# Expert weights fetched ahead in a one-core transformer block: 22 chunks for 18, expert one inside the ring, expert two outside

## What is computed

```python
def expert_choice_ffn(h, w_router, w_gate, w_up, w_down):
    b, n, d = h.shape
    cap = CAPACITY_FACTOR * n // N_EXPERTS
    aff = jax.nn.softmax((h @ w_router).astype(jnp.float32), axis=-1)
    gate, idx = lax.top_k(jnp.swapaxes(aff, 1, 2), cap)
    bidx = jnp.arange(b)[:, None, None]
    xe = h[bidx, idx]
    hid = jax.nn.silu(jnp.einsum('becd,edf->becf', xe, w_gate)) * jnp.einsum('becd,edf->becf', xe, w_up)
    ye = jnp.einsum('becf,efd->becd', hid, w_down) * gate[..., None].astype(h.dtype)
    return jnp.zeros_like(h).at[bidx, idx].add(ye)
```

## Time and profile before

| | us |
|---|---|
| median of three timed runs | 1674.55 |
| lowest, highest of them | 1671.48, 1675.87 |
| the profiled execution | 1667.71 |
| its span from first to last instruction | 1665.8 |

### The profile page before, as it was taken

The page is one execution under the profiler, slowest core; times in us unless marked ns, Lnnn a source line. Parts: engine busy times, 40 slices in busy tenths (PEclk is TensorE's granted clock), DMA queues, the critical chain, the costliest instruction groups (busy, mean ns, idle before and its releaser), DMA issues. The chain is left out here.

```text
span 1665.8 us, 26602 instructions
## 1 busy us (share of the span) xinstructions
PE 1429.2 (86%) x11146; PEld 1109.2 (67%) x11146; DVE 796.9 (48%) x1321; ACT 566.9 (34%) x821; POOL 25.2 (2%) x34
## 2 busy tenths in 40 slices
PE   5999998999968565565565599989999999999999
PEld 3889886678943121121121397549999999999999
DVE  4353336666722001000010578656776478777753
ACT  3432125675311000000000352654434366853341
POOL 1100000000000000000000000000000000200000
PEclk8999999999979877877787899999999999999999
DMA  9755447552599999999999854954545545444520
GB/s 396 310 227 219 154 168 312 213 217 102 218 382 365 428 428 428 428 427 428 427 428 428 360 220 147 383 212 144 186 178 181 188 163 177 177 172 183 178 102 26
DMA packets 48990, 437.69 MB, mean 263 GB/s; under 512 B 5232, under 2 KB 7664, under 8 KB 8304
## 3 DMA queue, kind: packets, MB, share of 16 engines
q1 hardware_dynamic: 47872, 430.99, 65.4%
q10 hardware_dynamic: 1008, 5.09, 0.7%
HBM read 435.00 MB, written 1.05 MB: 262 GB/s over the span
## 5 line engine op out<-in xcount | busy, mean ns | idle before, releaser
L796 PE MATMUL bank<-arena_r,ring_r 128*128 128x256 f32 (+1 forms) x5016 | 700.0, 285 | 12.5 <-DVE ring_end_r L1908 4.9
L796 PEld LDWEIGHTS bank<-arena_r,ring_r 128*128 128x128 f32 x5016 | 652.3, 191 | 28.3 <-issue 14.9
L1908 DVE TENSOR_TENSOR ring_r<-ring,ring_r 128x2048 fp32r<-128x2048 f32 (+1 forms) x108 | 246.0, 2280 | 154.0 <-ACT ring_r L1549 153.7
L1195 PE MATMUL bank<-ring,arena 128*32 128x512 f32 x1008 | 164.7, 785 | 117.0 <-DMA ring<-in_w 115.7
L1549 ACT ACTIVATE ring_r<-ring 128x2048 fp32r<-128x2048 f32 (+1 forms) x108 | 204.9, 1898 | 111.6 <-PE bank L796 102.9
L1195 PEld LDWEIGHTS bank<-ring,arena 128*32 128x32 f32 x1008 | 31.1, 127 | 237.4 <-DMA ring<-in_w 175.8
L796 PE MATMUL bank<-H_r,ring_r 128*128 128x256 f32 x816 | 182.4, 289 | 4.6 <-DVE H_r L1885 4.6
L796 PEld LDWEIGHTS bank<-H_r,ring_r 128*128 128x128 f32 x816 | 136.8, 195 | 8.2 <-issue 7.4
L2195 DVE TENSOR_TENSOR arena<-arena,bank 64x512 f32<-64x512 f32 x16 | 11.1, 691 | 261.4 <-ACT arena L1659 261.4
L1659 ACT ACTIVATE arena<-bank 64x512 f32<-64x512 f32 x16 | 9.4, 588 | 369.7 <-PE bank L1195 369.6
L796 PE MATMUL bank<-arena_r,ring_end_r 128*128 128x256 f32 (+1 forms) x400 | 114.3, 286 | 0.0
(11 more groups left out here) (296 smaller groups left out, 1406.0 us busy)
## 6 DMA issues: line engine op xcount, KB each, us to landing
ring<-in_w SPq DMA_DIRECT2D x93, 2048.0 KB, 25.6
ring<-in_w SPq DMA_DIRECT2D x171, 1024.0 KB, 4.9
ring_end<-in_w SPq DMA_DIRECT2D x45, 1024.0 KB, 4.9
ring<-in_bias ACTq DMA_DIRECT2D x1, 2048.0 KB, 12.4
H<-in_w SPq DMA_DIRECT2D x2, 1024.0 KB, 15.3
ring_end<-in_w SPq DMA_DIRECT2D x1, 2048.0 KB, 25.8
consts<-in_consts ACTq DMA_DIRECT2D x1, 1198.0 KB, 9.3
X<-in_x SPq DMA_DIRECT2D x1, 1024.0 KB, 5.7
```

Source lines behind the costliest of these rows:

```text
L796: i = nc.tensor.matmul(o, lhsT, rhs, start=start, stop=stop, skip_group_check=grouped)
L1195: last = matmul(bank[0][32 * j:32 * j + 32, :], x_e[:, k, CAP * e:CAP * e + CAP], columns(slot_of(c), j, 512), start=k == 0, stop=k == KT - 1)
L1908: v.tensor_tensor(r(lo), lo, r(hi), ALU.subtract).then_inc(lo_ready, 1)
```

## The change

The diff does these things.

- Four more homes, 18 to 21, all in `arena`; home 15 moves. To make room, the tiles of the routing and the gathers move within `arena` (`h_tok`, `y_tok`, `hot`, `hot_g`, `hot_t`, `aff`, `silu_g`, `hid`, `hid_t` and others).
- `EARLY` has ten entries for six. Chunks 0 to 11 of the expert stage (expert 0) lie in slots 0 to 11; chunks 12 to 21 (expert 1 without its last two) in slots 12, 13 and the eight homes; from chunk 22 on the ring turns, starting with slot 0.
- SP loads 22 chunks ahead. Six of them (homes 17 and 18 behind gate 11, the pair 10/11 and home 14 behind the last `att_t`, home 19 behind the last `att_o`) stand between the last `branch` chunk's load and the first `mix_out` chunk's. Homes 15 and 20 wait for the last `branch` product, 21 for the last `mix_out` product, 16 for the row sums as before.
- `x_e` becomes `x_first` (experts 0, 1), `x_next` (experts 2, 3) and two tiles `x_rest` (experts 4 to 15, half of the depth each, since they take the place of homes 21 and 19). `gather_next` (64 columns) stands behind each gate/up chunk of expert 1, `gather_rest` (384 columns) behind every second one of experts 2 and 3. The turn of the picks moves from expert 2 to expert 4.

The core of the diff:

```diff
-AHEAD = 2 * CAP
+AHEAD, NEXT = 2 * CAP, 4 * CAP
-SLOTS, CYCLE, HOMES = 14, 12, 4
+SLOTS, CYCLE, HOMES = 14, 12, 8
-EARLY = (12, 13) + tuple(range(SLOTS, SLOTS + HOMES))
-FIRST_CYCLE = FIRST_EXPERT + len(EARLY)
-FIRST_HOME = FIRST_EXPERT + CYCLE - len(EARLY)
+EARLY = (12, 13, 17, 18, 14, 19, 15, 20, 16, 21)
+FIRST_HOME = FIRST_EXPERT + CYCLE
+FIRST_CYCLE = FIRST_HOME + len(EARLY)
...
-            return {14: consts[:, 384:384 + CHUNK], 15: room(8448, CHUNK), 16: H[:, :, T:2 * T], 17: H[:, :, 0:T]}[s]
+            return {14: consts[:, 384:384 + CHUNK], 15: room(6144, CHUNK), 16: H[:, :, T:2 * T], 17: H[:, :, 0:T],
+                    18: room(13312, CHUNK), 19: room(11264, CHUNK), 20: room(4096, CHUNK), 21: room(0, CHUNK)}[s]
...
-        h_tok, x_e, y_tok = room(0, 2, D), room(2048, KT, EXPERTS * CAP), room(6400, 4, D)
+        h_tok, y_tok = room(8192, 2, D), room(3072, 4, D)
+        x_first, x_next = room(2048, KT, AHEAD), room(2560, KT, NEXT - AHEAD)
+        x_rest = [room(at, 4, 512 - NEXT) for at in (0, 11264)]
...
-            rounds(1)
-
+            first_mix = CHUNK_NO[("mix_out", 0)]
+            rounds(1, first_mix)
+
+            sp_eng.wait_ge(job_done, JOBS[("gate", 11)].no)
+            load_home(17, home(17))
+            load_home(18, home(18))
+            sp_eng.wait_ge(job_done, JOBS[("att_t", PAIRS - 1, 1)].no)
+            load_pair(10, pair_of(FIRST_EXPERT + 10))
+            load_home(14, home(14))
+            sp_eng.wait_ge(job_done, JOBS[("att_o", PAIRS // 2 - 1)].no)
+            load_home(19, home(19))
+            for c in range(first_mix, FIRST_EXPERT):
+                sp_eng.wait_ge(chunk_used, RING[c][2] + 1)
+                load(slot_of(c), w[c])
+
+            sp_eng.wait_ge(job_done, JOBS[("branch", 1, 2, 1)].no)
+            load_home(15, home(15))
+            load_home(20, home(20))
             sp_eng.wait_ge(merged_ready, 4)
-            load_home(14, home(14))
-            load_home(17, home(17))
-            for s in range(6, CYCLE, 2):
-                load_pair(s, pair_of(FIRST_CYCLE + s))
+            for s in (6, 8):
+                load_pair(s, pair_of(FIRST_EXPERT + s))
...
             load_pair(4, pair_of(FIRST_EXPERT + 4))
-            load_home(15, home(15))
+            sp_eng.wait_ge(job_done, JOBS[("mix_out", 3)].no)
+            load_home(21, home(21))
             sp_eng.wait_ge(job_done, JOBS[("row_sums",)].no)
             load_home(16, home(16))
...
                         if e == 1:
-                            gather_rest(k)
+                            gather_more("gather_next", k, AHEAD, NEXT)
+                        if e in (2, 3) and k % 2:
+                            gather_more("gather_rest", 4 * (e - 2) + k // 2, NEXT, 512)
...
                 hidden(0)
                 for k in range(1, KT, 2):
-                    takes(f(x_e[:, k, AHEAD:512], job(("gather_rest", k))[:, 0:512 - AHEAD], ACT.Identity,
-                            bias=mod[:, 24 + k, 0:1], scale=mod_a[:, 1, k:k + 1]), ("gather_rest", k))
+                    gathered("gather_next", k, x_next[:, k, :])
                 hidden(1)
+                for half in range(2):
+                    for k in (1, 3):
+                        gathered("gather_rest", 4 * half + k, x_rest[half][:, k, :])
+                    hidden(2 + half)
                 turn_picks()
-                with act.Fori(2, EXPERTS) as e:
+                with act.Fori(4, EXPERTS) as e:
                     hidden(e)
```

More of the change, by code:

```diff
@@ L409, in plan_jobs @@
                 last[b] = None
-            for n in range(KT):
-                add(("gather_rest", n), "act" if n % 2 else "dve", SUM_BANK + n % 4)
+            for name in ("gather_next", "gather_rest"):
+                for n in range(KT):
+                    add((name, n), "act" if n % 2 else "dve", SUM_BANK + n % 4)
             for t in range(2):
@@ L696, in pair_rounds @@
                 source = source.rearrange("r s (q x) -> r s q x", q=P)
-                for c in range(FIRST_CYCLE + CYCLE, FIRST_CYCLE + 2 * CYCLE, 2):
+                for c in range(FIRST_CYCLE, FIRST_CYCLE + CYCLE, 2):
                     sp_eng.wait_ge(chunk_used, RING[c + 1][2] + 1)
                     load_pair(slot_of(c), pair_of(c))
-                with sp_eng.Fori(2, full) as r:
+                with sp_eng.Fori(1, full) as r:
                     for i in range(CYCLE // 2):
@@ L709, in load_home, with rounds @@
             def load_home(s, source):
-                n = CYCLE - len(EARLY) + EARLY.index(s)
-                half = pair_of(FIRST_EXPERT + n - n % 2)[:, n % 2 * CHUNK:n % 2 * CHUNK + CHUNK]
+                n = EARLY.index(s)
+                half = pair_of(FIRST_HOME + n - n % 2)[:, n % 2 * CHUNK:n % 2 * CHUNK + CHUNK]
                 sp_eng.dma_start(source, half).then_inc(landed[s], 16)
-            def rounds(stage):
+            def rounds(stage, end):
                 first, slots, _ = RING_USE[stage]
-                n, end = len(slots), RING_USE[stage + 1][0]
+                n = len(slots)
                 full = (end - first) // n
@@ L761, in _ @@
                 load(s, w[FIRST_SECOND + i])
-            rounds(3)
+            rounds(3, len(CHUNKS))
             for p in range(4):
@@ L1186, in step_experts @@
                         in_sbuf(("gather", 1))
-                    if e == 2:
-                        in_sbuf(("gather_rest", KT - 2))
-                        in_sbuf(("gather_rest", KT - 1))
+                    if e in (2, 4):
+                        for k in (KT - 2, KT - 1):
+                            in_sbuf(("gather_next" if e == 2 else "gather_rest", k))
+                    if e == 4:
                         turn_picks()
@@ L2201, in hidden, with gathered @@
                     o.then_inc(ye_taken, 1)
+                def gathered(name, k, o):
+                    takes(v.tensor_scalar(o, job((name, k))[:, 0:o.shape[1]], mod_a[:, 1, k:k + 1], mod[:, 24 + k, 0:1],
+                                          ALU.mult, ALU.add), (name, k))
                 hidden(0, 0)
                 for k in range(0, KT, 2):
-                    takes(v.tensor_scalar(x_e[:, k, AHEAD:512], job(("gather_rest", k))[:, 0:512 - AHEAD],
-                                          mod_a[:, 1, k:k + 1], mod[:, 24 + k, 0:1], ALU.mult, ALU.add),
-                          ("gather_rest", k))
-                weigh_picks()
-                for u in range(1, 4):
-                    hidden(0, u)
+                    gathered("gather_next", k, x_next[:, k, :])
+                hidden(0, 1)
+                for half in range(2):
+                    for k in (0, 2):
+                        gathered("gather_rest", 4 * half + k, x_rest[half][:, k, :])
+                    if half:
+                        weigh_picks()
+                    hidden(0, 2 + half)
                 with dve.Fori(1, EXPERTS // 4) as i:
```

44 lines of the change are left out of this document (26 added, 18 removed).

## The result

| | before | changed |
|---|---|---|
| median of the runs, us | 1673.5 (1671.48 to 1675.87, 4 runs) | 1658.2 (1657.21 to 1662.21, 4 runs) |
| ratio, 95% interval | | 0.9919 (0.9899 to 0.9939) |
| the profiled execution, span, us | 1667.71, 1665.8 | 1662.21, 1660.4 |

Forecast was 1659.0. The medians lie 15.3 us apart, the two profiled executions only 5.5: that of before is faster than all four runs of its row, that of the changed kernel is the slowest of its four.

The account below looks back on a forecast made before the run. The expert stage was taken as bound by its weight stream at 428 GB/s. Terms 9.8 + 6.1 - 0.2 - 0.1 = 15.6 us off the median 1674.55 gave 1659.0; own range 1657 to 1661, 8-in-10 range 1655.5 to 1666.

Parts of the forecast that it names:

- What bounds it, and the pace: Expert stage: full DMA engines at 428 GB/s set its end; a pair of chunks costs 4.92 us.
- Four chunks ahead, 9.8 us: Start of the expert stage: 85 pairs instead of 87 remain at the same first refill, a gain of 9.8 us.
- Six early loads, 0: Loads between mixer weights: mix_out delayed about 5 us against at least 19 us of slack before ACT needs it, cost 0.
- Of 6.1 us of idle queue 5.9 come back: Refills during expert 1: seventh pair issued at 518.5, leaving a 0.2 us gap, so 5.9 of 6.1 us are regained.
- The second rival: Expert 1 too long for the queue: each us beyond 18.2 is empty queue; 6 us would give 1665; chance 0.10.
- A gap at 520: Queue of loads near 520 us: a gap standing there would show the forecast wrong.
- Three-step gather, 0: Experts 2 and 3: 6.1 us more gather work on PE, which catches the stream just before expert 4; cost 0.
- The seam, 0: From the last expert pair to the second half: later first chunk, one split before the norms; together +0.1 us, taken as 0.
- The moved split: Second split of the second half, now behind the norms: PE gets it 0.4 us after wanting it.
- The time: Whole kernel: a saving of 15.6 us, giving 1652.1 for the profiled execution and 1659.0 for the median.

Follow-up runs that it names:

- late_six: Changed kernel with the six loads among the mixer's weights taken out and issued behind them; median 1658.8 us, ratio 0.9924 to before.
- double_gather: Changed kernel with each 64-column gather product of expert 1 issued twice, values the same; median 1663.2 us, ratio 0.9942 to before.
- ring14_warm: Changed kernel with slots 12 and 13 in the turning ring, plus 8 and 18 unread filler products on PE during routing; median 1653.8 us, ratio 0.9884.
- warm: Changed kernel plus unread filler products on PE during routing, 8 before the affinities' wait and 18 before the slots' wait; median 1652.0 us, ratio 0.9879.
- ahead18: Changed kernel without the loads of homes 15, 20, 21 and 16, so 18 chunks ahead in the new order; median 1665.3 us, ratio 0.9956.
- the ring of fourteen: Changed kernel with slots 12 and 13 joined to the turning ring, still 22 chunks ahead; alone, medians 1653.4 and 1656.6 us in two jobs.
- after_third: Changed kernel run and traced a third time, no edit; median 1660.2 us, ratio 0.9927 to before.
- after_again: Changed kernel run and traced a second time, no edit; median 1661.6 us, ratio 0.9935 to before.
- warm_short: Changed kernel plus 6 and 12 unread filler products on PE before the affinities' and slots' waits; median 1651.2 us, ratio 0.9864 to before.
- ring14_warm_short: Changed kernel with slots 12 and 13 in the turning ring, plus 6 and 12 unread filler products on PE; median 1648.0 us, ratio 0.9862.

## Why the prediction was right, and the step that was not

- **What bounds it, and the pace**: right. 428 GB/s and 4.92 us for a pair hold in every trace.
- **Four chunks ahead, 9.8 us**: right. 9.4 between two kernels with hardly a shortfall, 9.1 to 10.6 over all traces once the shortfalls are deducted.
- **Six early loads, 0**: right, and by the slack that was named; the mix_out loads and the split behind them did not move. The value of their place is nothing too (`late_six`).
- **Of 6.1 us of idle queue 5.9 come back**: this is the term that failed. In the traces of the changed kernel 0.5 to 2.9 came back (shortfalls 5.5, 3.6 and 3.1 for 6.0). The forecast had expert 1 occupy PE from 500.18 to 518.2, 18.0 us; it takes 21.0 to 21.3. Two numbers went in too small. The gather's 0.44 us per chunk was read from a run of equal products; between the expert's own it is 0.59, 8 x 0.15 = 1.2 us in all. And the time from the first down product to expert 2 was taken from expert 0, 3.7 us, where the row of expert 1's own down products stood in the same group with 5.35 us, partly at half clock; the stretch 496 to 524 that the forecast gave for the clock ends just ahead of them, and the next one has 0.94. It takes 5.5 to 5.7 in the changed kernel, 1.8 to 2.0 us more. To this comes expert 0 at half clock, which in the first trace put 2.8 us in front of expert 1. The second rival named this mechanism (each us beyond 18.2 is a us of empty queue) and `double_gather` shows it one for one; it had deserved the higher chance, and the forecast the larger gap. A gap at 520 was one of the forecast's own signs of being wrong, and the gap stood there.
- **Three-step gather, 0**: right. PE catches the stream at expert 4 (568.81).
- **The seam, 0**: right with its working. The first split starts 6.92 us behind the last pair, forecast 6.6; the sum follows at 14.68, forecast 14.4 to 14.7. The moved split cost nothing, for 0.4.
- **The time**: the sum with the shortfalls as measured is 9.8 + 0.5 to 2.9 = 10.3 to 12.7 us. The comparisons gave 15.3, 11.2 and 12.9. So that 1659.0 came out within 0.8 us is in part luck: the failed term had 3.0 to 5.4 us too much, and the first comparison was the best of three, by a difference that its own traces do not show (5.4 us between the spans). With the 13.1 of their mean the forecast is 2.5 us too low, within the range given. What makes the medians of one kernel differ by 3.5 us between jobs is not settled; in the traces the differences lie ahead of the row turn (464.9 to 467.9), in expert 0's clock and behind the second half's first mixer product (708.9 to 712.2 us to the end), none of which the edits touch.

## What to carry to other kernels

When a kernel is bound by a stream of weights, fetching more ahead is worth the chunks' transfer time only if the buffers that turn are enough to bridge the stretch in which none comes free. Tiles filled once are good for the start and free nothing: write down, for each refill, when it is issued and when the queue runs dry (first issue + latency + pairs x pace), and look for the first that comes late. Two tiles moved from the kind that is used once to the kind that turns took the shortfall away in all four traces, for the same memory and the same number ahead. In the medians of the same job they were worth 8.2, 3.6 and, with the short fillers, 3.2 us, but nothing with the long ones (`ring14_warm` is 1.7 us slower than `warm`).

For the time of such a stretch take the rows of that stretch, with the engine's pauses in it, and not those of a neighbour at another clock.

## What the runs showed of the hardware

- On an idle queue a load of 2 MB counts as if its data started 1.6 to 1.8 us behind the issue at the full rate (13 traces, `late_six` left out). The first bytes come earlier and slower: in the changed kernel none in the first half microsecond behind 490.40, 131 and 328 GB/s in the next two.
- The sum of first data, pairs and shortfall puts the last byte 1.9 to 2.1 us ahead of PE's start on the last pair in the traces with a shortfall of 3 us or more, and 2.7 to 3.4 in `ahead18` and the four with the ring of fourteen. Why these have more is open.
- Without fillers PE goes into expert 0 at a granted clock of 0.50, but the point where it rises differs between executions of the same kernel (before 488 us in `after_third`, past 492 in the first trace), and expert 0's down products took 3.66 or 5.35 us. What decides it was not found.
- Behind the pause of 2.8 us (3.15 in the kernel before) ahead of expert 1's down products, in which nothing is awaited from DMA, the clock falls: 0.61 in 520 to 524 us of the changed kernel, 0.70 in `double_gather`, and these products take 5.0 to 5.4 us in all fourteen traces. The forecast went by the Trainium skill, "TensorE: Matmul & The Clock Gate", section "HAM oscillation — how this bites in real kernels", for waits for data, and took it that expert 1, its data all landed, stays at full clock; here it did not. That the wait for the other engines' evacuations brings the clock down was not tested, and it does not do so each time: ahead of expert 2's down products the pause is as long (2.19 us and 0.47), and they took 3.66 us in the changed kernel and 6.36 in `after_again`.
- The Trainium skill, "DMA: Bandwidth & Descriptors", section "Where 436 GB/s comes from", has about 358 GB/s as the limit from HBM. The changed kernel too moved 428 GB/s over 376 us, and the four chunks brought 9.4 us (9.1 to 10.6 over the traces), near the 9.8 that this rate gives, not 11.7.
- Eighteen products that nobody reads, in time that PE waited anyway (`warm_short`, `ring14_warm_short`), took 3.3 us off the gather behind them (7.06 to 3.76) and 1.4 to 2.9 off expert 0's first products.
